# A hybrid decoder step on one NeuronCore: router products spread between the output products of the tile three later

## What is computed

```
h = modulate(rmsnorm(x), shift1, scale1);  u = h @ w_in
mix = concat(pool_mixer(u[:, :512]), ssm_mixer(u[:, 512:])) @ w_out
x = x + g1 * mix
h2 = modulate(rmsnorm(x), shift2, scale2)
logits = h2 @ [router_w1 | router_w2] + bias      # 4 groups and 16 experts
x = x + g2 * hier_moe(h2, logits)                 # top group, top 2 of its 4 experts
y = rmsnorm(x, final_norm_g)
```

## Time and profile before

| | |
|---|---|
| median of 3 runs | 1302.78 us (1300.69 to 1307.26) |
| the profiled execution | 1300.7 us, span 1299.0 us |
| PE busy | 1086.8 us (84%) |
| PE, weight loads busy | 832.6 us (64%) |
| DVE busy | 761.1 us (59%) |
| ACT busy | 512.3 us (39%) |
| POOL busy | 257.1 us (20%) |
| mean granted TensorE clock | 0.907 of full speed |
| DMA | 244.75 MB, 188 GB/s over the span |

### The profile page before, as it was taken

How to read it: one execution, slowest core, us unless ns; L and a number is a source line. 1 busy time by engine, 2 the same in 40 slices (tenths; PEclk the granted TensorE clock), 3 DMA queues, 4 the chain that set the end, 5 groups by cost and what they waited for, 6 DMA issues and landing times. The chain is left out here.

```text
span 1299.0 us, 18067 instructions
## 1 busy us (share of the span) xinstructions
PE 1086.8 (84%) x5419; PEld 832.6 (64%) x5420; DVE 761.1 (59%) x1248; ACT 512.3 (39%) x759; POOL 257.1 (20%) x316
## 2 busy tenths in 40 slices
PE   4599999998488989989999824999999999999900
PEld 2266766765265668777788613777787777787700
DVE  2745566630589934475767667465566655555326
ACT  2523333311343225344444321455556545444315
POOL 0035344351140000000000001133233323233200
PEclk9699999998689989988898856999999999999955
DMA  9814646483774458465355453678789778765469
GB/s 295 305 38 123 193 116 196 122 288 98 213 112 131 137 180 259 127 232 162 144 185 195 146 195 120 204 210 224 219 272 284 213 216 223 225 155 108 74 202 394
DMA packets 175876, 244.75 MB, mean 188 GB/s; under 512 B 70903, under 2 KB 131015, under 8 KB 174743
## 3 DMA queue, kind: packets, MB, share of 16 engines
q1 hardware_dynamic: 151049, 180.32, 43.4%
q0 software_dynamic: 12528, 45.62, 15.4%
q10 hardware_dynamic: 12246, 18.14, 4.1%
HBM read 167.80 MB, written 75.84 MB: 188 GB/s over the span
## 5 line engine op out<-in xcount | busy, mean ns | idle before, releaser
L120 PE MATMUL experts_psGU<-weights_we_hi,experts_x_hi 128*128 (+1 forms) x344 | 144.7, 421 | 9.0 <-DVE experts_x_lo L2292 6.9
L121 PE MATMUL experts_psGU<-weights_we_hi,experts_x_lo 128*128 (+1 forms) x344 | 137.5, 400 | 0.0
L122 PE MATMUL experts_psGU<-weights_we_lo,experts_x_hi 128*128 (+1 forms) x344 | 137.5, 400 | 0.0
L120 PE MATMUL front_psM<-front_hT_hi,front_w_hi 128*128 128x512 f32 x256 | 105.7, 413 | 0.0
L2188 POOL DMA_INDIRECT acc_d<-experts_o_sb,experts_to_col x43 | 71.4, 1660 | 149.6 <-issue 64.4
L121 PE MATMUL front_psM<-front_hT_hi,front_w_lo 128*128 128x512 f32 x256 | 100.5, 393 | 0.0
L122 PE MATMUL front_psM<-front_hT_lo,front_w_hi 128*128 128x512 f32 x256 | 100.3, 392 | 0.0
L120 PEld LDWEIGHTS experts_psGU<-weights_we_hi,experts_x_hi 128*128 128x128 f32 x344 | 65.6, 191 | 34.9 <-issue 22.8
L2292 DVE TENSOR_TENSOR experts_x_lo<-experts_psX,experts_x_hi 128x1024 fp32r<-128x1024 f32 x44 | 53.9, 1225 | 45.5 <-ACT experts_x_hi L2224 45.5
L122 PEld LDWEIGHTS experts_psGU<-weights_we_lo,experts_x_hi 128*128 128x128 f32 x344 | 65.6, 191 | 15.7
L121 PEld LDWEIGHTS experts_psGU<-weights_we_hi,experts_x_lo 128*128 128x128 f32 x344 | 65.8, 191 | 12.2
(11 more groups left out here) (433 smaller groups left out, 2538.0 us busy)
## 6 DMA issues: line engine op xcount, KB each, us to landing
front_raw<-in_w_ada SPq DMA_DIRECT2D x32, 512.0 KB, 4.1
weights_we_raw<-in_exp_w_gate SPq DMA_DIRECT2D x16, 1024.0 KB, 6.0
weights_we_raw<-in_exp_w_up SPq DMA_DIRECT2D x16, 1024.0 KB, 12.5
weights_wd_raw<-in_exp_w_down SPq DMA_DIRECT2D x16, 1024.0 KB, 13.1
front_raw<-in_w_ada SPq DMA_DIRECT2D x8, 1024.0 KB, 11.8
front_xraw<-in_x_prompt SPq DMA_DIRECT2D x4, 2048.0 KB, 10.1
part_d<-middle_ev ACTq DMA_DIRECT2D x16, 512.0 KB, 3.2
middle_xt<-in_x_prompt SPq DMA_DIRECT2D x16, 512.0 KB, 4.8
```

What stands on the lines that cost most here:

```text
L120: pe.matmul(out, l_hi, r_hi, start=start, stop=False)
L121: pe.matmul(out, l_lo, r_hi, start=False, stop=False)
L122: return pe.matmul(out, l_hi, r_lo, start=False, stop=stop)
```

## The change

`product` takes the router's products in: behind each step q of half c of tile t comes the single router product number 4c + q of tile t-3. The waits of these products, now in `route_waits`, are called once a tile, ahead of the first product. The router of a tile so comes three tiles on instead of two; DVE's `logits` follow it, to t-3. `h2T` has a second buffer, laid over `ev1` as the first is over `ev0`, and ACT's copy waits for the router of two tiles back; the first copy into each waits for the stores that went out of the space below. Behind the loop the router blocks of tiles 14, 15 and 16 are left, in whole blocks.

```diff
--- before.py
+++ after.py
@@ -1110,7 +1110,7 @@
         rb = k.over("rb", [P, NR], "mp_hi", F32, KD * NR * 4)
         ss = k.over("ss", [P, 2, 4], "mp_hi", F32, KD * NR * 4 + 128)
         junk = k.over("junk", [P, D], "mp_lo", BF16)
-        h2T = k.over("h2T", [P, KD, P], "ev0")
+        h2T = [k.over("h2T0", [P, KD, P], "ev0"), k.over("h2T1", [P, KD, P], "ev1")]
         assert k.where["zs"] + 2 * SZ <= k.where["mraw"] and k.where["vt"] + 2 * SZ <= k.where["zs"]
 
         psX = k.ps(st, "psX", [P, 4, BLK])
@@ -1379,11 +1379,15 @@
                             pe.wait_ge(s["tmp"], t - 1)
                         pe.wait_ge(s["mlo"], QH * b + QH)
                     cs, j = slice(c * BLK, (c + 1) * BLK), t % TPB * P
+                    if c == 0 and t >= 3:
+                        route_waits(t - 3)
                     for q in range(QH):
                         mm = matmul3(pe, psO[0:n, u, cs], m_hi[b % 2][:, q, j:j + n], m_lo[b % 2][:, q, j:j + n],
                                      ws_hi[:, q, cs], ws_lo[:, q, cs], q == 0, q == QH - 1)
-                    if c == 1:
-                        mm.then_inc(s["mm"], 1)
+                        if c == 1 and q == QH - 1:
+                            mm.then_inc(s["mm"], 1)
+                        if t >= 3:
+                            route(t - 3, QH * c + q)
 
                 def turn(t):
                     u, n = t % 2, rows_of(t)
@@ -1394,16 +1398,18 @@
                         mm = pe.transpose(psH[:, q * P:q * P + n], h2[0:n, u, q * P:(q + 1) * P], idt[0:n, 0:n])
                     mm.then_inc(s["h_t"], 1)
 
-                def route(t):
-                    n = rows_of(t)
+                def route_waits(t):
                     if t == 0:
                         pe.wait_ge(s["rw_in"], 16 * 10)
                     else:
                         pe.wait_ge(s["lg_done"], t)
                     pe.wait_ge(s["h_ev"], t + 1)
-                    for q in range(KD):
-                        mm = pe.matmul(psR[0:n, :], h2T[:, q, 0:n], rw[:, q, :], start=q == 0, stop=q == KD - 1)
-                    mm.then_inc(s["r_mm"], 1)
+
+                def route(t, q):
+                    n = rows_of(t)
+                    mm = pe.matmul(psR[0:n, :], h2T[t % 2][:, q, 0:n], rw[:, q, :], start=q == 0, stop=q == KD - 1)
+                    if q == KD - 1:
+                        mm.then_inc(s["r_mm"], 1)
 
                 for p in range(PAIRS):
                     for i in range(2):
@@ -1448,13 +1454,16 @@
                     if t >= 2:
                         turn(t - 2)
                     product(t, 1)
-                    if t >= 2:
-                        route(t - 2)
                     if t + LEAD < GLUS:
                         gate(t + LEAD)
                 for t in (LAST - 1, LAST):
                     turn(t)
-                    route(t)
+                    route_waits(t - 1)
+                    for q in range(KD):
+                        route(t - 1, q)
+                route_waits(LAST)
+                for q in range(KD):
+                    route(LAST, q)
 
             @block.scalar
             def _(act):
@@ -1552,11 +1561,11 @@
                 def turned(t):
                     n = rows_of(t)
                     act.wait_ge(s["h_t"], t + 1)
-                    if t:
-                        act.wait_ge(s["r_mm"], t)
+                    if t >= 2:
+                        act.wait_ge(s["r_mm"], t - 1)
                     else:
-                        act.wait_ge(part_out[0], 16 * ((NT + 1) // 2))
-                    act.copy(h2T[:, :, 0:n], psH.rearrange("p (k n) -> p k n", k=KD)[:, :, 0:n]).then_inc(s["h_ev"], 1)
+                        act.wait_ge(part_out[t], 16 * ((NT + 1 - t) // 2))
+                    act.copy(h2T[t % 2][:, :, 0:n], psH.rearrange("p (k n) -> p k n", k=KD)[:, :, 0:n]).then_inc(s["h_ev"], 1)
 
                 for p in range(PAIRS):
                     for i in range(2):
@@ -1819,8 +1828,9 @@
                     if t == 2:
                         dve.wait_ge(s["rw_in"], 160)
                         scale_rows(1)
-                    if t >= 2:
-                        logits(t - 2)
+                    if t >= 3:
+                        logits(t - 3)
+                logits(LAST - 2)
                 logits(LAST - 1)
                 logits(LAST)
```

## The result

| | before | after |
|---|---|---|
| median | 1302.84 us (4 runs) | 1411.31 us (4 runs, 1408.84 to 1412.02) |
| the profiled execution | 1300.7, span 1299.0 | 1411.2, span 1409.4 |
| mean granted TensorE clock | 0.907 | 0.883 |

The change makes the kernel **8.2% slower**: the ratio is 1.0824, with a 95% interval of 1.0793 to 1.0855. Forecast were 1417 us, in a range of 1386 to 1450.

A forecast was written before the change was run, and what follows sets the result against it. DVE's pass is hidden under PE's product; the moved wait makes them take turns. Regular part 109.0, start 0, product 16 4.6, end 2.2, second buffer 0: +115.8 us on 1300.7, 1416.5, forecast as 1417, range 1386 to 1450.

The forecast's parts named there:

- The round: Output loop, product to product: PE and DVE take turns, so a full interval becomes 21.1 us against 11.8.
- Products and turn with the router passes: PE's part of each interval: both product halves and turn 6.6 us, plus eight spread router products 2.1.
- Low clock: Product behind PE's 7 us stop in each tile: starts at the lower clock for 5.2 us, costing 2.4.
- DVE's pass: DVE's work on one tile, from residual to next residual, now wholly inside each interval: 9.7 us.
- Logits to PE: End of each interval: DVE writes the logits and PE takes them up, 0.2 us.
- The count: Product 4 to product 16, twelve intervals: sum 250.9 us against 141.95, so +109.0.
- The start: Loop up to product 4: no shift, 0 us, between -0.5 and +2.
- Product 16: Last tile's product, with the step to DVE: 11.2 us instead of 6.64, so +4.6.
- The end: Behind DVE's pass over tile 16: three router blocks instead of two, 6.8 to 8.3 us against 5.42, taken as +2.2.
- The clock that does not come back: Rival for the output loop: clock stays low within a tile, 5.6 us more per product, 1490 us; chance 0.10.
- The clock that does not fall: Rival for the output loop: no low clock behind stops, 13 x 2.4 us less, 1386 us; chance 0.10.
- The faster kernel: Rival for the output loop: spreading removes PE's stops and most low-clock loss, 1281 us; chance 0.02.

The follow-up runs named there:

- e1: Kernel before plus one wait: from tile 4 on, the first output product waits for the logits of the tile before the last; 1401.1 us.
- e2: Changed kernel with DVE's logits at the head of its pass over a tile instead of its end; 1271.3 us.
- e3: Changed kernel with DVE's logits behind the residual, in mid-pass, instead of at the end; 1311.4 us.
- e4: Changed kernel with products whose results are thrown away put into PE's stop behind the gate of tiles 3 to 15; 1383.3 us.
- e6: Kernel before with DVE's logits of tile t-3 at the head of the pass over tile t, router block kept whole; 1301.9 us.
- e5: Kernel before with DVE's logits, still of tile t-2, moved from the end of the pass to behind the residual; 1277.0 us.
- e11: e2 with the router's 8 products as a block behind the tile's product instead of spread, repeat run; 1274.5 us.

## Why the prediction was right

**The bound.** That DVE closes a pass just when PE closes the product, and that the product hides the pass, is what the whole forecast rests on. The wait alone (e1) and the moved logits (e2, e3) show it. Product 5 starts 21.0 us behind product 4, where less than 15 would have refuted it.

**The round.** Forecast 21.1 us, measured 20.7 in the round shown and 20.7 to 21.4 in tiles 4 to 10 (tile 6, with the split, apart). By terms:

- Products and turn with the router passes: 6.6 + 2.1 forecast. The round above takes 5.11 us for three groups at the low level and 5.40 for the rest; at the upper level it would be 8 x 0.92 + 0.83 less the last router pair (0.23), plus the 0.16 by which a product's record outlasts its pace, 8.1. The passes so cost 1.5 on the path and not 2.1. A pair takes 0.225 us, as in the block, and the eighth pair stands behind the last product, where the residual no longer waits for it. That was overlooked. The Trainium skill ("TensorE: Matmul & The Clock Gate", "Part 3: Packing small matmuls — row/col tiling") says in its list of what overlaps that loads overlap a running product only where the row group differs. That is not borne out here either: a pair with its two loads, all on full rows, costs 0.225 us, where two loads of 0.20 one behind the other would take 0.4.
- Low clock: 2.4 forecast, 2.3 measured by the filled stop. The rule of the Trainium skill (the same page, "HAM oscillation — how this bites in real kernels") has each burst behind a long wait start low. The trace agrees: 13 of 13 products did.
- DVE's pass: 9.7 forecast, 9.73 measured.
- Logits to PE: 0.2 forecast, 0.44 measured (605.54 to 605.98). The length of the stop is not the reason: behind the 0.60 us of e4 and the 1.13 of e3 it is 0.43 too. The waiting router product before took 0.22 (606.58 to 606.80); why a wide product takes twice that is open.

The misses in the round, passes 0.6 too high and this step 0.2 too low, partly cancel.

**The count.** Twelve rounds gave 250.9 forecast and 248.1 measured; the tile with the split of a whole block took 1.6 more (1.4 forecast), tile 15 took 19.2 (19.4).

**Start and end.** The start was 0 forecast and 0.2 measured, if the earlier begin of the loop is left out. Product 16 was put at +4.6 and gave +2.7: the passes cost less, the low level lasted only some 3 us, and a group takes 0.86 us with its 64 rows and not 0.92. The end was put at +2.2 and gave +3.1, just above the range that was given (6.8 to 8.3 less 5.42, so 1.4 to 2.9): block 15 ran at the low level throughout (3.6). The two misses partly cancel. For the profiled execution 1416.5 us were forecast and 1411.2 measured: 2.8 of the difference are the rounds, some 0.8 start and end, and 1.9 only that the loop began sooner. That the total is so close owes something to luck, since a pass too dear and a step too cheap stood in the same sum.

**The second buffer** at nothing: measured alone, nothing.

**The rivals.** The clock that does not come back (1490) and the clock that does not fall (1386) both fell: it comes back within each product, after 5.1 us in the round shown, the case of the dense stream, and after 6.4 at most. The faster kernel (1281) needed the awaited logits to lie ahead of the product. The change does not do that, and e2, which makes it so, runs in 1271. The regular stretch was sized about right (8.4 + 11 us forecast, 141.95 - 123.58 = 18.4 measured); what this rival left out is the start, where product 4 of e2 comes 10.6 us sooner behind the first residual.

What the forecast did not see: in the profiles the spreading has a small worth of its own, 4 to 7 us of the loop, buried under the 110 of the wait. Nor did it see that the stop of 0.35 us in the kernel before already cost some 2 us in tiles where the clock fell behind it.

## What to carry to other kernels

When a block of work is cut up and spread into an earlier one, its wait moves to the head of that earlier work. Ask where the engine that answers stands at that moment: here PE asked one product too early, and a stop of 0.35 us a tile became one of 7. Move the answer too, so far ahead that it is there when it is asked for. In the changed kernel the step from the end of the pass to its head did it; in the kernel before, the step from the end to behind the residual was worth about 2% without any spreading. A head that is the same moment as the end of the pass before (e6) gains nothing.

## What the runs showed of the hardware

- Behind the stops of 7.2 to 10.3 us every product of the change began at the lower clock, and the upper one came back after some 3 us (tile 16) to 6.4 us (tile 7). Filling the stops with products whose results are thrown away made the kernel 28 us faster; with stops of 0.6 us in most tiles the clock averaged 0.98.
- Stops of 1.13 us in each of seven tiles left the granted clock at 1.00 over 86 us; stops of 2.65 us brought it to 0.82.
- A stop of 0.35 us ahead of the block of router products was followed by the lower clock in the gate of 512 columns in all seven such tiles of e6 (0.61 over 4.43 us in tile 5), and in four of seven before. In e5, with no stop ahead of the block, tile 5's gate ran at 1.00 and took 2.86 us.
- Eight router products as a block, with no stop around them, let the clock fall in tiles whose gate has 64 columns (0.82 to 0.93 from 662 us on in e11, two rounds of 11.1 us); the same products spread singly did not (1.00, 9.5 us).
